# A two-block transformer kernel: the last 14 taps of the last convolution chunk weighed on ScalarE and summed on GpSimd

## The reference

```python
u = conv_a * jax.nn.sigmoid(conv_gate)            # 512 tokens x 512 channels
u = causal_depthwise_conv(u, conv_w, conv_b)      # 31 taps a channel
u = jax.nn.silu(layernorm(u, conv_ln_g, conv_ln_b))
qk = jax.nn.silu(causal_depthwise_conv(jnp.concatenate([q, k], axis=-1), qk_conv_w, qk_conv_b))   # 4 taps
ht = mlstm_chunkwise(...)                         # 4 heads of 128
hm = jax.nn.sigmoid(o) * ht                       # then normed head by head
y = jnp.concatenate([u, hm], axis=-1)
return jnp.einsum("bse,ed->bsd", y, w_out)
```

## Time and profile before

| what | us |
|---|---|
| median of 3 runs | 2052.38 (2051.47 to 2054.06) |
| profiled execution, its time | 2054.98 |
| profiled execution, its span | 2053.7 |
| TensorE busy | 1824.7 |
| GpSimd busy | 992.7 |
| VectorE busy | 863.6 |
| ScalarE busy | 432.7 |
| last dense tile of the input projection ends | 1377.3 |
| last tap of the convolution starts | 1428.16 |

### The profile page before, as it was taken

One profiled execution on the slowest core, in us unless ns is written; L12 is line 12 of the kernel. 1 busy time (PEld: TensorE's weight loads), 2 busy tenths in 40 slices (PEclk: granted clock), 3 DMA queues, 4 the chain that ended last, 5 costly groups with the idle time before them and its releaser, 6 DMA issues.

```text
span 2053.7 us, 27415 instructions
## 1 busy us (share of the span) xinstructions
PE 1824.7 (89%) x9686; PEld 1287.1 (63%) x9686; DVE 863.6 (42%) x1256; ACT 432.7 (21%) x794; POOL 992.7 (48%) x536
## 2 busy tenths in 40 slices
PE   5999999989999899999999798996877978969783
PEld 4888888877776578888888666664642423323331
DVE  5444443410254567444444489877341111111113
ACT  3111100100244432111100143551321211111112
POOL 5888887767544278888888523321211111101101
PEclk9999999999999999999999999997868988988897
DMA  3333363423221123333333222210579999999983
GB/s 126 97 97 93 105 262 98 141 79 98 66 62 52 32 85 95 97 93 101 92 109 98 72 60 64 72 52 21 212 287 412 374 408 402 410 415 398 413 358 133
DMA packets 56977, 346.00 MB, mean 168 GB/s; under 512 B 8474, under 2 KB 8858, under 8 KB 44896
## 3 DMA queue, kind: packets, MB, share of 16 engines
q1 hardware_dynamic: 44640, 315.12, 42.1%
q10 hardware_dynamic: 7968, 19.46, 2.6%
q0 software_dynamic: 4320, 10.78, 1.5%
HBM read 475.06 MB, written 19.66 MB: 241 GB/s over the span
## 4 chain that ended last, share of the span: by engine, by line
PE 70%; DMA 13%; DVE 11%; ACT 3%; issue 1%; POOL 1%; SPq 0%; DVEq 0%; ACTq 0%; POOLq 0%
PE bank L460 31%; DMA big<-w_up_in 13%; PE bank L431 12%; PE bank L1760 7%; PE bank L692 4%; PE bank L1266 3%; DVE big L1043 3%; PE bank L1778 2%; PE bank L479 2%; PE bank L1376 2%; PE bank L1786 1%; PE bank L610 1%; DVE state L1028 1%; PE bank L670 1%; PE bank L1678 1%
## 5 line engine op out<-in xcount | busy, mean ns | idle before, releaser
L277 POOL TENSOR_TENSOR weights_hi_parts<-ring,ones 128x1024 fp32r<-128x1024 f32 (+1 forms) x176 | 356.6, 2026 | 304.7 <-PE bank L460 139.1
L279 POOL TENSOR_TENSOR ring_parts<-ring,weights_hi_parts 128x1024 fp32r<-128x1024 f32 (+1 forms) x176 | 473.9, 2693 | 13.8
L460 PE MATMUL bank<-attention_buffers_parts,weights_hi_parts 128*128 128x512 f32 x832 | 329.4, 396 | 27.9 <-POOL ring_parts L279 17.6
L460 PE MATMUL bank<-state_parts,weights_hi_parts 128*128 128x512 f32 x832 | 326.8, 393 | 0.0
L460 PE MATMUL bank<-attention_buffers_parts,ring_parts 128*128 128x512 f32 x832 | 326.7, 393 | 0.0
L1760 PE MATMUL bank<-big,work 128*32 128x512 f32 x1440 | 231.7, 685 | 54.5 <-DMA big<-w_up_in 54.4
L431 PE MATMUL bank<-big_parts,weights_hi_parts 128*128 128x512 f32 x704 | 217.1, 389 | 1.2 <-POOL ring_parts L279 1.2
L460 PEld LDWEIGHTS bank<-attention_buffers_parts,weights_hi_parts 128*128 128x128 f32 x832 | 158.1, 190 | 64.6 <-POOL ring_parts L279 17.6
L864 POOL TENSOR_TENSOR ring_parts<-ring,weights_hi_parts 128x1024 fp32r<-128x1024 f32 x32 | 81.0, 2534 | 234.1 <-ACT weights_hi_parts L861 234.1
L1860 POOL TENSOR_TENSOR small<-small 128x1 f32<-128x1 f32 x51 | 9.7, 190 | 381.3 <-DVE small L1683 381.3
L460 PEld LDWEIGHTS bank<-state_parts,weights_hi_parts 128*128 128x128 f32 x832 | 158.3, 190 | 33.4 <-issue 0.8
(11 more groups left out here) (377 smaller groups left out, 2827.1 us busy)
## 6 DMA issues: line engine op xcount, KB each, us to landing
big<-w_up_in SPq DMA_DIRECT2D x54, 2048.0 KB
ring<-wdense_in SPq DMA_DIRECT2D x176, 512.0 KB, 3.6
state<-w_down_in SPq DMA_DIRECT2D x37, 2048.0 KB
big<-w_gate_in SPq DMA_DIRECT2D x36, 2048.0 KB
attention_buffers<-w_gate_in SPq DMA_DIRECT2D x18, 2048.0 KB
ring<-w_down_in SPq DMA_DIRECT2D x18, 2048.0 KB
ring<-wff_in SPq DMA_DIRECT2D x32, 704.0 KB, 4.1
y_rows<-big ACTq DMA_DIRECT2D x1, 8192.0 KB, 28.0
```

The costliest lines, as they stand in the source:

```text
L277: po.tensor_tensor(hi, raw, ones[:, 0:1].to_broadcast([128, words]), ALU.mult).then_inc(PO.sem, 1)
L279: po.tensor_tensor(lo, raw, hi.bitcast(F32), ALU.subtract) \
L460: m = pe.matmul(out, x, y_, start=j + n == 0, stop=j == len(pairs) - 1 and n == len(ts) - 1)
```

## The change

For chunk 3 `conv_taps` stops after 16 of its 30 VectorE taps. A new generator in `background`, `shared_taps`, begins once the last dense tile has been issued. It weighs the other 14 taps on ScalarE (L1066 in the new numbering), the first into `total`, the others by turns into two buffers `scaled`, all in `att`; GpSimd adds them to `total` (L1069), and VectorE adds `total` to the chunk (L1078). `convolved[3]` is that last add. The weighing of tap n waits for `added[n]`, the list having two entries ahead of the first add.

```diff
--- before.py
+++ after.py
@@ -956,7 +956,7 @@
     scored, summed_up, taken, var_read, split, split_u, silus = {}, {}, {}, {}, {}, {}, {}
     v2_ready, rows_ready, sig_read, stats_read = [], [], [selectors], {}
     floored = {}
-    next_taps, x_ready = [], []
+    next_taps, x_ready, own_taps, SHARED_TAPS = [], [], [], 14
     dense_done, rows_at, taps_at, tick_at = [], [], {}, []
 
 
@@ -1037,13 +1037,46 @@
         last = AC.step(ac.activation(chunk(ym, c), u_pad[:, c * PU:c * PU + T], ACT.Identity,
                                      scale=col("conv_w", c * CONV_W), bias=col("conv_b", c)))
         began = est("ac", 0.65)
-        for j in range(1, CONV_W):
+        for j in range(1, CONV_W - (SHARED_TAPS if c == 3 else 0)):
             src, w, dst = u_pad[:, c * PU + j:c * PU + j + T], col("conv_w", c * CONV_W + j), chunk(ym, c)
             DV.wait(last, gated[c] if j == 1 else None)
             last = DV.step(dv.scalar_tensor_tensor(dst, src, w, dst, ALU.mult, ALU.add))
             clk["dv"] = max(clk["dv"], began) + 0.85
             yield
-        convolved[c] = last
+        if c < 3:
+            convolved[c] = last
+        else:
+            own_taps.append(last)
+
+    def wait_for_taps():
+
+        while not dense_done:
+            yield 0
+        yield from shared_taps()
+
+    def shared_taps():
+
+        total, scaled = att[:, 0:T], (att[:, T:2 * T], att[:, 2 * T:3 * T])
+        AC.wait(gated[3], ring_freed[23])
+        added, at = [None, None], 0.0
+        for n in range(SHARED_TAPS):
+            j = CONV_W - SHARED_TAPS + n
+            AC.wait(added[n] if n > 1 else None)
+            d = scaled[n % 2] if n else total
+            a = AC.step(ac.activation(d, u_pad[:, 3 * PU + j:3 * PU + j + T], ACT.Copy, scale=col("conv_w", 3 * CONV_W + j)))
+            if n:
+                PO.wait(a, added[-1])
+                added.append(PO.step(po.tensor_tensor(total, total, d, ALU.add)))
+            else:
+                PO.wait(a)
+            at = max(at, est("ac", 0.7)) + 1.1
+            yield at - 1.0
+        while not own_taps:
+            yield 0
+        yield at
+        DV.wait(added[-1], own_taps[0])
+        convolved[3] = DV.step(dv.tensor_tensor(chunk(ym, 3), chunk(ym, 3), total, ALU.add))
+        est("dv", 0.8)
 
 
     weights = [W(3), W(4)[:, 0:384], W(5)[:, 0:256], W(4)[:, 384:512]]
@@ -1288,6 +1321,8 @@
                 ALU.add, ALU.mult))
             est("dv", 0.8)
             long_taps.append(conv_taps(n))
+            if n == 3:
+                background.append([wait_for_taps(), 0.0])
         elif kind == "o":
             dense_read[bank] = opened["o", n] = AC.step(ac.activation(o_gate[n], banks[bank][:, :], ACT.Sigmoid,
                                                                       bias=col("b_o", n)))
```

## The result

The changed kernel takes 2059.85 us in the median against 2053.64 us before, 22 runs of each, of which one of the changed kernel (3054.33 us, at a mean granted clock of 0.555) is left out of all comparisons. The ratio is 1.0028, with a 95% interval from 1.0021 to 1.0035. That is 4.3 to 7.2 us more, 5.75 in the middle; the two medians are 6.2 us apart. The forecast was 6.3 us more, a median of 2058.7. The profiled execution has a span of 2057.4 us.

A forecast was written before the change was run, and what follows sets the result against it. Two nearly equal paths, VectorE's taps and 14.77 us of TensorE matmuls, bound the kernel behind head 3. Delays carried along to the reciprocal (6.0 us late) and product gave 2052.38 + 6.3 = 2058.7 us, range 2055.0 to 2062.6.

The forecast's parts named there:

- Nothing to gain but 0.45 us: At the `conv_norm` product: TensorE idles only 0.45 us before it, so taking all taps away gains no more.
- The first adds meet L1138: 1.0 us: Last mLSTM head: early GpSimd adds block VectorE's tap and L1138, making TensorE's restart 1.0 us late.
- Weighings 5 and 6 hold the square: 4.65 us: ScalarE's queue: two weighings between split L861 and head 3's square L1151 make the square 4.65 us late.
- the third rival: GpSimd adds 5 to 8, 12 and 13 each wait 0.48 us more: +9.2, 2061.6 us; chance 0.08.
- The lock: VectorE and GpSimd: each add blocks VectorE instructions with two SBUF inputs until it ends; sum +6.3 us, not +2.7.
- L1163 4.0 us late, the reciprocal 6.0: Head 3: variance matmul takes 1.7 us, L1163 is 4.0 us late; taps meeting adds make the reciprocal 6.0 late.
- From the second tile on: +0.3: TensorE works 14.77 us, then the final add: the reciprocal's 6.0 us delay becomes +6.3 at the product.
- What the product moves by, the end moves by: After the `conv_norm` product: everything later waits for it, so the end shifts by the same +6.3 us.
- The signs: Profile after: square 4 to 5 us after L1181, second tile about 1420, idle above 9.41, taps 1.3 to 1.9 us.
- The rival of an expert stage that forgives 2 us of the shift: Expert weight stream hides up to 2.1 us: +4.2, 2056.6 us; chance 0.15 together with no lock.
- The rival without a lock: Adds don't block taps, only ScalarE's queue delays: +2.7, 2055.1 us; chance 0.15 together with part of the shift forgiven.
- The other side: Head 3 isn't held up, the meeting point comes sooner: 0.45 us less, 2051.9; chance 0.05 including other gains.

The follow-up runs named there:

- left_out: Kernel before with the last 14 taps of chunk 3 left out and nothing in their place; ratio 0.9919, tokens' values differ.
- six_shared: Changed kernel with 6 shared taps instead of 14; one run, no ratio, head 3's square 25.97 us after the zero.
- seven_shared: Changed kernel with 7 shared taps instead of 14; one run, no ratio, head 3's square 30.01 us after the zero.
- memset: Changed kernel with each GpSimd add replaced by a memset of 1280 columns, 13 taps missing from the output; ratio 0.9985.
- two_ahead: Changed kernel, but a weighing waits only for the last reader of its own buffer, the add two before it; ratio 1.0002.
- delay5: Kernel before with seven more VectorE tap-like instructions, result unused, behind chunk 3's last tap, nothing shared; ratio 1.0016.
- memset_two_ahead: Changed kernel with memsets for the adds and weighings waiting only for their own buffer, 13 taps missing from the output; ratio 0.9977.
- five_shared: Changed kernel with 5 shared taps instead of 14, all weighed ahead of the split of tile 26; ratio 1.0002.
- hold_12: Changed kernel with 12 shared taps, weighings waiting only for their own buffer, VectorE's taps held back while head 3 is finished; ratio 0.9994.
- before_hold: Kernel before, nothing shared, with VectorE's long taps held back until head 3 is finished; ratio 1.0005.

## Why the prediction was right

- *Nothing to gain but 0.45 us.* Shown by left_out: 0.53, for the last 14 taps.
- *The first adds meet L1138: 1.0 us.* Measured 1.07 at TensorE's restart (1394.90 - 1375.42 against 1395.78 - 1377.37). With memsets in place of the adds L1171 takes 0.69 us and the restart is 18.43 us after the zero, no later than before.
- *Weighings 5 and 6 hold the square: 4.65 us.* Measured 4.65. That 6 and its wait are the cause is shown by six_shared against seven_shared; that the order alone, without the lock, costs some 3.2 us is borne out by memset, 3.05. The longer waits of the third rival did not come: the square stands where the sum without them has it.
- *The lock.* Shown by memset against the changed kernel: 3.4 us at the product (58.68 - 55.32), and by taps that run at their usual speed beside memsets; a small part of the 3.4 is that a memset took 1.16 us and an add left alone 1.26. The Trainium skill's page "SBUF — State Buffer" (section "Who interferes with whom") states both halves of this, that the shared port pair is held for the whole instruction, and that a VectorE instruction with two SBUF inputs contends with a GpSimd instruction that reads SBUF but not with one that only writes it; the memset run agrees (2.07 us for three taps).
- *L1163 4.0 us late, the reciprocal 6.0.* Measured 4.37 and 5.58. The variance matmul took 2.09 us, not 1.7; the taps beside adds 7 and 8 took 3.18 us in the chain, not 3.95, since the add for 7 had only 0.4 us left when they began.
- *From the second tile on: +0.3.* Measured +1.3 (6.88 - 5.58). This is the term that was mis-sized. TensorE's work took 15.38 us, not 14.77: its clock came back after 6.1 us instead of 4.8, a difference that I had costed at nothing. That doesn't follow from the idle stretch ahead, which was 9.40 us, as long as before and not the 10 expected; why the clock came back later stays open. The other path came later with it, since its split L861 waits for TensorE (8.69 us after the second tile instead of 8.09), and the adds for 12 and 13 took 1.27 and 1.26 us instead of 1.18; so TensorE waited 1.14 us for the final add, not 0.75. In the sum at the product, 0.4 us too much at the reciprocal and 1.0 too little behind it cancel in part (6.3 against 6.88): there the closeness is partly luck.
- *What the product moves by, the end moves by.* True of the trace up to the gather (6.88 and 6.92), but not a law: in two_ahead 2.9 us and in delay5 1.2 us of the delay came back before the gather, at another clock. At the end the two profiles of the changed kernel are 5.65 and 6.14 us late, less than at the product. The prediction had named that as a sign of being wrong; it is within the scatter of the expert stage. That the forecast of 6.3 lay within the measured 4.3 to 7.2 owes something to this: in both profiles of the changed kernel the stage kept its clock, while three of the 21 runs took 2053.4 to 2053.7 us, no longer than before.
- *The signs.* L1184 started 4.10 us after L1181 ended, the second tile 42.16 us after the zero (1419.5 on the clock of before), the final add ended 0.88 us after TensorE's own arrival: as named. Not as named were TensorE's idle stretch, 9.40 us and not above 9.41, and the three taps beside adds 7 and 8, 1.09 us each and not 1.3 to 1.9.
- The rival of an expert stage that forgives 2 us of the shift isn't borne out. From the gather to the end, six kernels with all taps and the gather within 1.2 us of before took 534.1 to 537.9 us, and the four profiles with it 3.3 to 7.0 us late 535.1 to 536.3. About 1 us stays open. The rival without a lock falls with memset against the changed kernel. The other side, a head that isn't held up, did happen in memset_two_ahead, by taking away both causes, and brought 0.29 us.

## What to carry to other kernels

Before work is moved off an engine, look at what its last instruction meets: here another engine had 14.8 us of its own work in the same 15 us, and leaving the work out altogether gained half a microsecond. A helper chain across two queues puts its waits in front of whatever those queues carry: count, for each added instruction, what stands behind it and what it waits for, since one instruction of 0.7 us cost 4 us at its place. And GpSimd work with SBUF inputs here didn't run beside VectorE's two-input work but between it.

## What the runs showed of the clock

TensorE's granted clock falls to 0.50 in the idle stretches and comes back while it works, but not after a fixed stretch of work. From the start of the second tile it stayed at 0.50 for 4.8 us before, for 6.1 in the changed kernel, 5.5 in memset, 3.8 in seven_shared, 3.7 in five_shared and 2.9 in six_shared, after idle stretches of 9.41, 9.40, 8.21, 8.20, 9.95 and 10.87 us. The idle time alone doesn't order them (before and changed, memset and seven_shared).

Further on, the stage between the product and the first gather took two lengths in the main, with two kernels apart. In before, the changed kernel (twice), five_shared, six_shared, seven_shared, hold_12 and the two memset kernels it took 88.0 to 88.3 us, in two_ahead and before_hold 85.3, in delay5 87.0 and in left_out, whose tokens' values differ, 83.5. The windows of the 16 us in which the routing's first matmuls run tell them apart (columns as in the earlier trace rows); before, then the changed kernel, then two_ahead:

```profile
1484.00:1500.00 16.00, 13.53 (x78) 13.16 (x77) 7.41 (x36) 8.05 (x15) 1.90 (x3) 0.59 0.96 385
```

```profile
1489.00:1505.00 16.00, 13.51 (x78) 13.13 (x77) 7.39 (x36) 8.07 (x15) 1.89 (x3) 0.59 0.98 390
```

```profile
1486.60:1502.60 16.00, 9.72 (x83) 9.25 (x81) 10.06 (x54) 10.49 (x19) 2.42 (x4) 0.89 0.94 372
```

The clock there is 0.59, 0.59 and 0.89, and TensorE needs 13.5, 13.5 and 9.7 us for the work in the window. Which of the two comes up isn't ordered by how late the product is (two_ahead 4.1, before_hold 3.8, delay5 5.6 on the one side; seven_shared 3.3, memset 3.5, changed 6.9 on the other), and what decides it stays open. Over 21 runs of the changed kernel the mean clock and the time go together: 2053.4 to 2053.7 us at a clock of 0.943 in three runs, 2057.95 to 2063.8 us at 0.934 to 0.939 in the others. The three short ones have no profile, so that they owe it to the stage above is likely, not shown. A ratio near 1.002 in this kernel can be the clock's as well as the edit's, and the places in the trace had to carry the argument.
